# Expert tiles of a mixture-of-experts step: both kinds of transposes ahead of gate-up, steps of an unused tile left out

## What is computed

```python
def hierarchical_moe(h, w_group, b_group, w_router, b_router, w_gate, w_up, w_down):
    ...
    gates = jnp.sum(jax.nn.one_hot(expert_id, N_EXPERTS, dtype=jnp.float32) * top_w[..., None], axis=1)
    hg = jnp.einsum('td,edf->tef', t, w_gate)
    hu = jnp.einsum('td,edf->tef', t, w_up)
    a = jax.nn.silu(hg) * hu * gates[..., None].astype(t.dtype)
    y = jnp.einsum('tef,efd->td', a, w_down)
```

## Time and profile before

| what | value |
|---|---|
| time, median of 3 runs | 1089.63 us (1085.09 to 1090.03) |
| profiled execution | 1089.73 us, its span 1087.9 us |
| PE busy | 931.1 us, 86% of the span |
| DVE busy | 462.5 us, 43% |
| ACT busy | 405.0 us, 37% |
| POOL busy | 158.5 us, 15% |
| scatters (L1704) | 27, of 1899 ns each on POOL |
| weight pieces rounded (L1735, L1790) | 48 of 1909 ns on ACT, 48 of 2292 ns on DVE |

### The profile page before, as it was taken

The page is one execution under the profiler, slowest core; times in us unless marked ns, Lnnn a source line. Parts: engine busy times, 40 slices in busy tenths (PEclk is TensorE's granted clock), DMA queues, the critical chain, the costliest instruction groups (busy, mean ns, idle before and its releaser), DMA issues. The chain is left out here.

```text
span 1087.9 us, 13921 instructions
## 1 busy us (share of the span) xinstructions
PE 931.1 (86%) x4691; PEld 758.8 (70%) x4691; DVE 462.5 (43%) x625; ACT 405.0 (37%) x656; POOL 158.5 (15%) x192
## 2 busy tenths in 40 slices
PE   4999968999999987899999999844999999898940
PEld 3779847778865766587888887633787787776830
DVE  3341193432113446572322222446564556675314
ACT  5442201410014657552211111612465556665313
POOL 3210000000010110000000000402023332323315
PEclk9989988999999989999999999975999999999975
DMA  7312020180015794620000000862789898989548
GB/s 237 136 39 73 20 84 20 74 332 1 1 55 205 284 339 139 237 81 6 1 1 1 1 1 1 344 256 90 233 251 274 263 287 251 337 290 292 105 106 331
DMA packets 40844, 165.24 MB, mean 152 GB/s; under 512 B 4987, under 2 KB 5387, under 8 KB 32058
## 3 DMA queue, kind: packets, MB, share of 16 engines
q1 hardware_dynamic: 28738, 112.74, 28.3%
q0 software_dynamic: 11456, 49.45, 16.1%
q10 hardware_dynamic: 576, 2.10, 0.5%
HBM read 133.04 MB, written 31.34 MB: 151 GB/s over the span
## 5 line engine op out<-in xcount | busy, mean ns | idle before, releaser
L1790 DVE TENSOR_TENSOR e_Wl<-raw,e_Wh x48 | 109.9, 2292 | 83.6 <-ACT e_Wh L1735 83.3
L529 PE MATMUL ps<-a_wh,a_hTh 128*128 128x512 f32 x288 | 116.3, 404 | 2.6 <-DVE a_hTl L487 1.3
L1735 ACT CAST e_Wh<-raw x48 | 91.6, 1909 | 67.0 <-issue 58.8
L531 PE MATMUL ps<-a_wl,a_hTh 128*128 128x512 f32 x288 | 114.1, 396 | 0.0
L530 PE MATMUL ps<-a_wh,a_hTl 128*128 128x512 f32 x288 | 114.1, 396 | 0.0
L1617 PE MATMUL ps<-e_Wh,e_xTh 128*128 x224 | 91.7, 409 | 0.0
L1618 PE MATMUL ps<-e_Wl,e_xTh 128*128 x224 | 89.0, 397 | 0.0
L1619 PE MATMUL ps<-e_Wh,e_xTl 128*128 x224 | 88.6, 396 | 0.0
L1704 POOL DMA_INDIRECT x_rows<-e_y,dst x27 | 51.3, 1899 | 200.0 <-DMA x_rows<-e_y,dst 125.0
L529 PEld LDWEIGHTS ps<-a_wh,a_hTh 128*128 128x128 f32 x288 | 55.7, 193 | 14.4 <-DVE a_wl L367 1.6
L531 PEld LDWEIGHTS ps<-a_wl,a_hTh 128*128 128x128 f32 x288 | 55.2, 192 | 11.9
(11 more groups left out here) (309 smaller groups left out, 1869.9 us busy)
## 6 DMA issues: line engine op xcount, KB each, us to landing
raw<-in_w_e SPq DMA_DIRECT2D x48, 1024.0 KB
t_raw<-in_w_att SPq DMA_DIRECT2D x64, 256.0 KB, 4.2
a_raw<-in_w_mix SPq DMA_DIRECT2D x20, 512.0 KB, 6.1
t_ring<-in_kc POOLq DMA_DIRECT2D x8, 1024.0 KB, 6.4
t_ring<-in_vc POOLq DMA_DIRECT2D x8, 1024.0 KB, 8.7
x_rows<-x SPq DMA_DIRECT2D x10, 512.0 KB, 4.9
a_xin<-in_x SPq DMA_DIRECT2D x9, 512.0 KB, 5.1
x<-in_x SPq DMA_DIRECT2D x9, 512.0 KB, 6.0
```

Of the source, the lines that this page charges most:

```text
L529: pe.matmul(out, hTh[:, c, own], h, start=(c == 0), stop=False)
L531: last = pe.matmul(out, hTh[:, c, own], l, start=False, stop=(c == KC - 1))
L1735: act.copy(Wh[:, ds(off + q * PIECE, PIECE)], raw[:, ds(off + q * PIECE, PIECE)]).then_inc(hi_ok[q], 1)
L1790: dve.tensor_tensor(Wl[:, at], raw[:, at], Wh[:, at].bitcast(F32), ALU.subtract).then_inc(lo_ok[q], 1)
```

## The change

In step s the order is now:

- PE: turn(s + 1), turn_a(s - 1), gate_up(s), down(s - 1).
- ACT: rows of s + 1, activation of s - 1, silu(s), pieces 0 and 1 of s + 2, y of s - 1, piece 2 of s + 1.
- DVE: rows of s + 1, rest of the activation of s - 1, activation product of s, pieces 0 and 1 of s + 2, piece 2 of s + 1.

The work is the same for each used tile. From step 17 on, what belongs to tile s or to turning s + 1 stands behind a branch of its own on whether tile s is used, inside the branch on tile s - 1. So PE reads the table three times in such a step, not twice, and ACT and DVE read `started` three times, not once; pieces 0 and 1 share their reads of `starts`, which saves one read on DVE and, where a tile starts an expert, two on ACT. POOL and SP are not changed.

```diff
@@ -1661,17 +1661,14 @@
         def buffer(n):
             return (n + 1) % 2 * ESZ

-        def tile_steps(eng, emit):
-            def unless_empty(s, like):
-                with eng.If(started(eng, s - 1) >= 1):
-                    emit(s, like)
+        def tile_steps(eng, step):
             for s in range(NTILE + 1):
                 if s < MIN_TILES:
-                    emit(s, s)
-                else:
-                    unless_empty(s, s)
+                    step(s, ExitStack)
+                    continue
+                with eng.If(started(eng, s - 1) >= 1):
+                    step(s, lambda: eng.If(started(eng, s) >= 1))

         @block.sync
         def _(sp):
@@ -1746,33 +1743,36 @@
             round_piece(0, (2,))
             round_piece(1, (0, 1))

-            def step(s, like):
-                if like + 1 < NTILE:
-                    round_xT(s + 1, like + 1)
-                if like < NTILE:
-                    act.wait_ge(gu_ps, s + 2)
-                    if like >= 1:
-                        act.wait_ge(a_ok, s)
-                    act.activation(sg[:, :], ps[:, 2 + like % 2, 0:FE], ACT.Silu).then_inc(sg_ok, 1)
-                if like + 2 < NTILE:
-                    round_piece(s + 2, (0,))
-                if like < NTILE:
-                    act.wait_ge(aT_ps, s + 1)
-                    if like >= 2:
-                        act.wait_ge(dn_ps, 2 * (s - 1) + 2)
-                    act.copy(aTh[like % 2][:, :, :], ps[:, 6, 0:FC * P].rearrange("p (c t) -> p c t", t=P)).then_inc(
-                        aTh_ok, 1)
-                if like + 2 < NTILE:
-                    round_piece(s + 2, (1,))
-                if like >= 1:
-                    par = (like - 1) % 2
-                    act.wait_ge(dn_ps, 2 * (s - 1) + 3)
-                    if like >= 3:
-                        act.wait_ge(y_st, 16 * (s - 2))
-                    act.copy(y[:, par, 0:512], ps[:, 4, :]).then_inc(y_ok, 1)
-                    act.wait_ge(dn_ps, 2 * (s - 1) + 4)
-                    act.copy(y[:, par, 512:D], ps[:, 5, :]).then_inc(y_ok, 1)
-                if like + 1 < NTILE:
+            def round_aT(s):
+                act.wait_ge(aT_ps, s + 1)
+                if s >= 2:
+                    act.wait_ge(dn_ps, 2 * s)
+                act.copy(aTh[s % 2][:, :, :], ps[:, 6, 0:FC * P].rearrange("p (c t) -> p c t", t=P)).then_inc(aTh_ok, 1)
+            def copy_y(s):
+                for h in range(2):
+                    act.wait_ge(dn_ps, 2 * s + 3 + h)
+                    if s >= 2 and h == 0:
+                        act.wait_ge(y_st, 16 * (s - 1))
+                    act.copy(y[:, s % 2, h * 512:(h + 1) * 512], ps[:, 4 + h, :]).then_inc(y_ok, 1)
+            def step(s, if_started):
+                if s + 1 < NTILE:
+                    with if_started():
+                        round_xT(s + 1, s + 1)
+                if s:
+                    round_aT(s - 1)
+                if s < NTILE:
+                    with if_started():
+                        act.wait_ge(gu_ps, s + 2)
+                        if s:
+                            act.wait_ge(a_ok, s)
+                        act.activation(sg[:, :], ps[:, 2 + s % 2, 0:FE], ACT.Silu).then_inc(sg_ok, 1)
+                if s + 2 < NTILE:
+                    round_piece(s + 2, (0, 1))
+                if s:
+                    copy_y(s - 1)
+                if s + 1 < NTILE:
                     round_piece(s + 1, (2,))
             tile_steps(act, step)
             act.copy(sg[0:1, 0:1], ident[0:1, 0:1])
@@ -1802,24 +1802,27 @@
             rest_of_piece(0, (2,))
             rest_of_piece(1, (0, 1))

-            def step(s, like):
-                if like + 1 < NTILE:
-                    rest_of_xT(s + 1, like + 1)
-                if like < NTILE:
-                    dve.wait_ge(sg_ok, s + 1)
-                    if like >= 1:
-                        dve.wait_ge(aT_ps, s)
-                    dve.scalar_tensor_tensor(out=a[:, :], in0=sg[:, :], scalar=GATE[:, s:s + 1], in1=ps[:, 2 + like % 2, FE:2 * FE],
-                                             op0=ALU.mult, op1=ALU.mult).then_inc(a_ok, 1)
-                if like + 2 < NTILE:
-                    rest_of_piece(s + 2, (0,))
-                if like < NTILE:
-                    dve.wait_ge(aTh_ok, s + 1)
-                    dve.tensor_tensor(aTl[like % 2][:, :, :], ps[:, 6, 0:FC * P].rearrange("p (c t) -> p c t", t=P),
-                                      aTh[like % 2][:, :, :].bitcast(F32), ALU.subtract).then_inc(aT_ok, 1)
-                if like + 2 < NTILE:
-                    rest_of_piece(s + 2, (1,))
-                if like + 1 < NTILE:
+            def rest_of_aT(s):
+                dve.wait_ge(aTh_ok, s + 1)
+                dve.tensor_tensor(aTl[s % 2][:, :, :], ps[:, 6, 0:FC * P].rearrange("p (c t) -> p c t", t=P),
+                                  aTh[s % 2][:, :, :].bitcast(F32), ALU.subtract).then_inc(aT_ok, 1)
+            def step(s, if_started):
+                if s + 1 < NTILE:
+                    with if_started():
+                        rest_of_xT(s + 1, s + 1)
+                if s:
+                    rest_of_aT(s - 1)
+                if s < NTILE:
+                    with if_started():
+                        dve.wait_ge(sg_ok, s + 1)
+                        if s:
+                            dve.wait_ge(aT_ps, s)
+                        dve.scalar_tensor_tensor(out=a[:, :], in0=sg[:, :], scalar=GATE[:, s:s + 1], in1=ps[:, 2 + s % 2, FE:2 * FE],
+                                                 op0=ALU.mult, op1=ALU.mult).then_inc(a_ok, 1)
+                if s + 2 < NTILE:
+                    rest_of_piece(s + 2, (0, 1))
+                if s + 1 < NTILE:
                     rest_of_piece(s + 1, (2,))
             tile_steps(dve, step)

@@ -1871,27 +1874,29 @@
             pe.sem_inc(dn_ps, 2)
             turn(0, 0)

-            def step(s, like, last, this):
-                if like + 1 < NTILE:
-                    turn(s + 1, like + 1)
-                if like < NTILE:
-                    gate_up(s, like, this)
-                if like >= 1:
-                    down(s - 1, like - 1, last)
-                if like < NTILE:
-                    turn_a(s, like)
             last = None
             for s in range(NTILE + 1):
                 if s < MIN_TILES:
+                    turn(s + 1, s + 1)
+                    if s:
+                        turn_a(s - 1, s - 1)
                     this = started(pe, s)
-                    step(s, s, last, this)
+                    gate_up(s, s, this)
+                    if s:
+                        down(s - 1, s - 1, last)
                     last = this
-                else:
-                    last = started(pe, s - 1)
-                    with pe.If(last >= 1):
-                        step(s, s, last, started(pe, s) if s < NTILE else None)
+                    continue
+                last = started(pe, s - 1)
+                with pe.If(last >= 1):
+                    if s + 1 < NTILE:
+                        with pe.If(started(pe, s) >= 1):
+                            turn(s + 1, s + 1)
+                    turn_a(s - 1, s - 1)
+                    if s < NTILE:
+                        this = started(pe, s)
+                        with pe.If(this >= 1):
+                            gate_up(s, s, this)
+                    down(s - 1, s - 1, last)


 def combine_block(nc, io, keep, x2_dram):
```

## The result

The changed kernel takes 1096.81 us (median of 6 runs, 1094.72 to 1100.94), before took 1089.77 on the same terms (6 runs, 1085.09 to 1092.27): ratio 1.0062, 95% interval 1.0037 to 1.0087. It is slower by about 7 us, where 1086.9 was forecast and 1095.5 was the upper end of the range. The profiled execution took 1095.28 (span 1093.5), so its trace shows 5.5 of the 7 us.

What follows compares the result with a forecast made beforehand. PE's own work was taken as the bound, with 24.2 us of waits above it in the loop. Loop +0.2 and end -3.0 gave -2.8 us: 1086.9 us forecast, range 1078 to 1095.5.

Steps and rivals of the forecast that it cites:

- the end: Blank tile 27's transposes and gate-up go; last scatter starts at 1044.8 against 1047.83, -3.0 us.
- What is late next: the rest of the activation (L1818, aTl): DVE's aTl ready +9.7 us after the silu against 9.08 needed; PE waits 0.8 in one-piece steps, 3.3 in three-piece.
- the sum of the loop: Expert loop: tiles 0 to 16 +0.6, 16 to 24 +1.0, 24 to 26 -1.4; +0.2 us in all.
- follows 1.00 behind: ACT's third weight piece starts 1.00 us behind the second copy of y, at +3.70 from the silu, two table reads included.
- the upper end of 1.2 for slow reads: One-piece steps: PE's wait for aTl is up to 1.2 us where table reads take longer; 0.8 taken.
- full waits: Steps 15, 19 and 21, ahead of the down product: PE waits 3.3 us each for aTl, 9.9 together.
- The clock: Each 3.3 us wait ahead of a down product costs another 1.5 us at the lower PE clock, three times.
- Reads and branches: Extra table reads from step 17 on PE, ACT and DVE: nothing taken, upper bound 0.8 in ten steps, 8 us.
- Rival 2: PE's sequencer exposes reads ahead of row transposes, 0.8 us in each of ten steps: 1095; chance 0.14.
- Rival 1: aTl is in time where only one weight piece is rounded, taking 10 x 0.8 away: 1079; chance 0.20.
- The far jumps: Step 27: PE's two jumps over transposes and gate-up take 2.05 us instead of 0.3: 1087.9; chance 0.08.

Runs made afterwards that it cites:

- order alone: The new order in every step without the inner branches, tile 27 still worked on, against before: 1095.45 us, ratio 1.0058.
- skip alone: Before's order, with PE, ACT and DVE branching from step 17 on whether tile s is used, against before: 1086.65 us, ratio 0.9978.
- both edits: Changed kernel with last activation ahead of next rows and piece 2 behind them, on ScalarE and VectorE: 1086.69 us, ratio 0.9966 to before.
- the changed kernel with five buffers: Changed kernel with five buffers for x rows in place of four: 1095.64 us, ratio 1.0050 to before.
- the kernel with the last activation first: Changed kernel with aTh and aTl of the last activation ahead of the next rows' xTh and xTl: 1084.92 us, ratio 0.9954 to before.
- the fastest kernel: Changed kernel with last activation, next rows, then piece 2 on ScalarE and VectorE, and five x-row buffers: 1074.16 us, ratio 0.9862 to before.

## Why the prediction was wrong

The forecast was -2.8 us: +0.2 for the loop and -3.0 for the end. In the trace the loop is +11.0 and the end -2.8. The step that failed is "What is late next: the rest of the activation (L1818, aTl)" with the sum of the loop built on it. The mechanism was right: TensorE waits for aTl ahead of the down products. Its size was wrong, taken too small in the terms below.

**Piece 2 "follows 1.00 behind" the second copy of y.** In the earlier trace rows both halves of the down products were long done when ScalarE had finished aTh, so its sequencer handed out the two copies together, at the start of the first. Its first read for piece 2 began at 800.4, beside the first copy, and piece 2 started 1.48 us behind that copy (800.36 to 801.84). The 1.00 is counted from the second copy, which ran 0.48 later. In the new order the sequencer stands at the wait for the second half and reads only when it has handed out the second copy: the read began at 819.9, and piece 2 came 1.49 behind it (819.91 to 821.40). Every later member of the chain is late by the difference: piece 2 +4.22 from the silu where +3.70 was counted, its rest +6.44 (+5.92), rest of the rows +8.65 (+8.12), aTl +9.78 (+9.26). The seven waits that were counted came to 1.01 to 1.48 us where 0.8 was taken, and those tiles to 1.3 to 1.76 us above the period. Taking the reads away from that place gives back 4.4 us of the 7 by the ratios (6.6 by the medians, of different groups). I had named the upper end of 1.2 for slow reads and not seen that the change itself brings the reads into the open.

**The first tile, and what a wait costs beside itself.** The seven one-piece waits were joined by an eighth that was not counted, ahead of tile 0's down products, the longest: 1.95. Together 10.1 us, and each interval is another 0.3 above the wait in it, so that the stretch stands 12.2 us above the period, not 6.5.

**Three pieces and the clock.** The first two full waits were sized right: 3.39 (tile 15) and 3.16 (tile 19) against 3.3. The third, tile 21, was 1.36; tiles 16 and 20, taken at 0.4, waited 1.29 and 1.24; tiles 17 and 22, taken at 0.8, 1.09 and 0.62. With 0.47 and 0.48 of "issue" that is 13.1 us against 12.3: the sum of the waits was nearly right because its errors cancel, which is luck. The clock cost 1.7 and 2.6 us in the two down products behind the long waits, where 1.5 was taken three times, so 4.3 against 4.5. The other 3.5 of the 20.9 us above the period lie beside the waits, 0 to 0.8 an interval, and had no term in the forecast.

**Reads and branches, taken at nothing.** Some 1.2 of those 3.5 us are theirs, the longer way from the pair of transposes to gate-up. Against order alone the changed kernel lost 1.7 us from tile 16 to tile 26, in single executions. This is within the upper bound of 8 that was named, and small beside the order.

**The end.** -2.8 us against the forecast's -3.0, but by another road, so this agreement is luck too. The last tile of the changed kernel:

```profile
1045.38 0.39 PE L1859 MATMUL ps<-ident,e_a 128*128 128x128 f32 x2
...
1046.44 1.59 POOL L1701 DMA_INDIRECT x_rows<-e_y,dst  x1 [6.57 <-ACT e_y L1757]
...
1047.63 0.37 ACT L1750 CAST e_aTh<-ps 128x256 fp32r<-128x256 f32 x1 [1.46 <-issue]
1048.03 0.42 DVE L1807 TENSOR_TENSOR e_aTl<-ps,e_aTh 128x256 fp32r<-128x256 f32 x1 [4.28 <-ACT e_aTh L1750]
...
1048.87 0.49 PE L1617 MATMUL ps<-e_Wh,e_aTh 128*128 x1 [3.11 <-DVE e_aTl L1807]
...
1054.37 1.59 POOL L1701 DMA_INDIRECT x_rows<-e_y,dst  x1 [5.06 <-ACT e_y L1757]
```

The forecast had the last scatter wait for the landing of the one before, and took this for the road of before too. It was not: in the earlier trace rows the last scatter is released by ScalarE's y, and the one before, issued at 1038.56 with the 7.4 of the earlier trace rows, had landed at 1046.0, 1.9 ahead of it. In the changed kernel it waits for y as well: aTh stands behind both copies of y of the tile before and the reads of the table (1.46 us of "issue"), TensorE then waits 3.11 us for aTl, and its products run at 0.63 of the clock, 4.61 us where 2.7 was counted. The scatter before was issued at 1046.44 and its landing took 6.4 us; it was down at 1052.8, 1.5 ahead of the last. The road through the landing was counted 1.0 us too long, and the one through y 2.7 too short (the last copy ended 11.4 us behind the start of tile 25's down products where 8.7 was counted). The last scatter came 11.7 us behind that start where 11.5 was forecast. In skip alone, where aTl is made earlier, the last scatter does wait for the landing, and the same stretch is 17.8 us, 2.3 less than before.

**What held.** ScalarE's wait for the pair went, the waits for x rows behind the first step went inside the new ones, and the last gate-up is that of tile 26. Rival 2 named nearly the right time, 1095, for a reason that the trace refutes: it wanted 0.8 us of "issue" ahead of the row transposes in ten steps, and there were 0.47 and 0.48 in two. Rival 1 was that aTl comes in time and gives 1079; the kernel in which it nearly always does (both edits) took 1086.7, since the x rows were late next, and 1074.2 once they were not. The far jumps did not decide: the 3.11 us of TensorE's wait in the last step end with aTl.

The sum, with the trace's numbers in the same places: +6.3 +5.1 -0.4 -2.8 = +8.2 from the first gate-up to the last scatter; less 1.6 for the earlier start and 1.0 for the shorter way between the last scatter and the first load of the combine stage, 5.6: the difference of the spans.

## What to carry to other kernels

When an operation moves, write down for its result the whole queue of the engine that makes it, from the last event that is fixed, and see which of the members nobody waits for: here the rest of the next rows (1.22 us) stood ahead of the rest of the last activation, and swapping them turned +0.6% into -0.5%. A distance between two instructions taken from the old trace holds only if the engine's sequencer stands at the same wait in the new order; reads of registers and branches that ran beside another instruction come out into the open when a late wait moves ahead of them. Where a faster order meets the next chain (here gathers issued behind scatters) try the buffer with the order, since the buffer alone may show nothing: the fifth was worth nothing clear of the noise with the old order and 11 us with both edits.

## What the runs showed of the hardware

- A wait of some 3 us ahead of the down products was followed by 4.6 to 5.5 us at a granted clock of 0.63, 0.50 and 0.63; waits of 1.0 to 1.5 us in the first 16 tiles left it at 0.99 over the stretch. So the price of such a wait was 4.8 to 5.8 us, wait and slow products together. It does not always come: in the changed kernel with five buffers the products behind a wait of 3.13 us ran at 1.00 and took 2.87 us, and those behind waits of 3.29 and 3.23 at 0.62 and 0.50 (4.39 and 5.28 us).
- A register read on ScalarE took 0.45 us of its sequencer with the median load of 0.28 us (single loads up to 1.13), and two reads with their branch held back the next instruction by 0.91 to 1.66 us (the latter at 820.33 in the kernel with the last activation first, where one load took 1.08).
- The scatters of the first 16 tiles, behind the first three, stood on the mean 9.8 us apart in before, 9.9 in the changed kernel, 9.6 with the last activation first and 9.5 in the fastest kernel, where TensorE took 9.35 us a tile; single distances were 6.9 to 12.8 in before. Most were released by the landing of the last (12, 12, 13 and 12 of them). That every member of this chain waits for the one before did not show that it sets the pace.
